# Gated mixer: mixing interleaved with the second half of u and with the output projection, which takes its first eight contraction tiles for all eight column groups at once

## The reference

```python
def gmlp_mixer(h, w_in, ln_g, ln_b, ws, bs, w_out):
    B, S, _ = h.shape                                # 1, 256, 1024
    z = jax.nn.gelu(h @ w_in, approximate=False)     # w_in: 1024 x 4096
    u, v = z[..., :GM_HALF], z[..., GM_HALF:]        # 2048 each
    v = layernorm(v, ln_g, ln_b)
    vc = v.reshape(B, S // GM_CHUNK, GM_CHUNK, GM_GROUPS, GM_GROUP_DIM)   # chunks of 128 tokens, 8 groups of 256
    mixed = jnp.einsum('gpq,bnqgc->bnpgc', ws, vc) + bs.T[None, None, :, :, None]
    return (u * mixed.reshape(B, S, GM_HALF)) @ w_out    # w_out: 2048 x 1024

x = x + g_m * gmlp_mixer(h_lat, ...)
x = x + g_f * squared_relu_mlp(modulate(x, norm_ffn_g[i], sh_f, sc_f), ffn_w1[i], ffn_w2[i])
```

## Time and profile before

| | us |
|---|---|
| median of 3 timed runs | 991.48 |
| lowest and highest of them | 991.28, 992.29 |
| span of the profiled execution, first to last instruction | 987.1 |
| median less span | 4.4 |
| PE busy in the span | 943.5 |

### The profile page before, as it was taken

One profiled execution on the slowest core, in us unless ns is written; L12 is line 12 of the kernel. 1 busy time (PEld: TensorE's weight loads), 2 busy tenths in 40 slices (PEclk: granted clock), 3 DMA queues, 4 the chain that ended last, 5 costly groups with the idle time before them and its releaser, 6 DMA issues.

```text
span 987.1 us, 19548 instructions
## 1 busy us (share of the span) xinstructions
PE 943.5 (96%) x6882; PEld 871.3 (88%) x6882; DVE 706.0 (72%) x1132; ACT 538.3 (55%) x921; POOL 309.0 (31%) x272
## 2 busy tenths in 40 slices
PE   5988989999999999999979999999999999999996
PEld 5877556799999999988969999999999879899996
DVE  4997778678988777897886688555555773475664
ACT  3464655565765444654634666654444761674645
POOL 1942122237997111120051288640110000330012
PEclk9898999999999999999979999999999998999999
DMA  9856175168878777788615676555555332255521
GB/s 351 292 182 239 42 226 171 47 218 309 309 271 275 284 267 279 244 324 283 225 61 171 234 256 214 186 176 190 171 192 182 130 95 98 86 172 173 169 87 43
DMA packets 57052, 195.60 MB, mean 198 GB/s; under 512 B 6303, under 2 KB 9791, under 8 KB 56736
## 3 DMA queue, kind: packets, MB, share of 16 engines
q1 hardware_dynamic: 55312, 192.36, 56.7%
q0 software_dynamic: 1680, 2.44, 1.1%
HBM read 192.65 MB, written 1.07 MB: 196 GB/s over the span
## 4 chain that ended last, share of the span: by engine, by line
PE 85%; DVE 9%; ACT 2%; issue 2%; DMA 1%; POOL 0%; SPq 0%; DVEq 0%; ACTq 0%
PE bank L526 24%; PE bank L527 24%; PE bank L528 24%; DVE w_lo L1576 2%; PE bank L791 1%; PE bank L925 1%; PE bank L951 1%; PE bank L624 1%; PE bank L782 1%; DMA x<-x_in 1%; PE bank L824 1%; PE bank L633 1%; PE bank L879 1%; DVE ada_raw L1678 1%; DVE ada_raw L1591 1%
## 5 line engine op out<-in xcount | busy, mean ns | idle before, releaser
L1576 DVE TENSOR_TENSOR w_lo<-raw,w_hi 128x1024 fp32r<-128x1024 f32 (+1 forms) x261 | 340.0, 1304 | 108.0 <-ACT w_hi L1146 106.1
L1146 ACT ACTIVATE w_hi<-raw 128x1024 fp32r<-128x1024 f32 (+1 forms) x261 | 272.4, 1044 | 174.4 <-PE bank L528 166.4
L526 PE MATMUL bank<-act_hi,w_hi 128*128 128x258 f32 (+1 forms) x872 | 251.5, 288 | 0.0
L527 PE MATMUL bank<-act_lo,w_hi 128*128 128x258 f32 (+1 forms) x872 | 248.0, 284 | 0.0
L528 PE MATMUL bank<-act_hi,w_lo 128*128 128x258 f32 (+1 forms) x872 | 247.5, 284 | 0.0
L526 PEld LDWEIGHTS bank<-act_hi,w_hi 128*128 128x128 f32 x872 | 166.1, 190 | 3.3 <-issue 2.8
L527 PEld LDWEIGHTS bank<-act_lo,w_hi 128*128 128x128 f32 x872 | 166.1, 190 | 1.0 <-issue 1.0
L528 PEld LDWEIGHTS bank<-act_hi,w_lo 128*128 128x128 f32 x872 | 166.1, 190 | 0.0
L528 PE MATMUL bank<-hid_hi,w_lo 128*128 128x256 f32 x512 | 143.4, 280 | 0.0
L526 PE MATMUL bank<-hid_hi,w_hi 128*128 128x256 f32 x512 | 142.8, 279 | 0.0
L527 PE MATMUL bank<-hid_lo,w_hi 128*128 128x256 f32 x512 | 142.8, 279 | 0.0
(11 more groups left out here) (349 smaller groups left out, 1812.7 us busy)
## 6 DMA issues: line engine op xcount, KB each, us to landing
raw<-weights SPq DMA_DIRECT2D x247, 512.0 KB, 3.6
ada_raw<-ada SPq DMA_DIRECT2D x88, 512.0 KB, 4.8
raw<-weights SPq DMA_DIRECT2D x14, 384.0 KB, 4.3
ada_more<-ada SPq DMA_DIRECT2D x8, 512.0 KB, 6.4
bias<-bias_by_distance SPq DMA_DIRECT2D x1, 2048.0 KB, 9.1
x<-x_in SPq DMA_DIRECT2D x1, 1024.0 KB, 7.3
ctx<-ctx_in SPq DMA_DIRECT2D x1, 1024.0 KB, 9.5
out<-result SPq DMA_DIRECT2D x4, 256.0 KB, 2.7
```

The lines of the kernel that those rows point to most:

```text
L526: pe.matmul(dst, w[0], a[0], start=start, stop=False)
L527: pe.matmul(dst, w[0], a[1], start=False, stop=False)
L1146: act.activation(w_hi[:, slot, 0:width_of(c)], raw[:, slot, 0:width_of(c)], ACT.Copy).then_inc(weight_hi, 1)
L1576: dve.tensor_tensor(w_lo[:, slot, 0:w], raw[:, slot, 0:w], w_hi[:, slot, 0:w].bitcast(fp32), ALU.subtract).then_inc(weight_lo, 1)
```

## The change

The 16 mixing tiles no longer stand in a block of their own. Tiles 0 to 7 are mixed in pairs behind groups 4 to 7 of `gm_u1`, tiles 8 to 15 one by one behind the first eight steps of `gm_out`. Mixing uses banks 4 to 7 in turn, and PE's tile t waits for DVE's tile t-4. `gm_out` is cut in two: in its first eight steps, step k takes contraction tile k for all eight output groups at once (a new order of `gm_w_out` in the chunks, `chunks_in_halves`), the groups lying two to a bank in banks 0 to 3; in its last eight steps, step 8+g takes the contraction tiles 8 to 15 of group g. `gm_out` is no longer a hardware loop. DVE makes four bias tiles in each of the steps j = 0 to 3 and two mixed tiles in each of the steps 4 to 7. The mixed tile t goes to slot (t + 8) mod 16 of `s_hi` and `s_lo`, so that tiles 0 to 7 don't write what `gm_u1` still reads.

```diff
+        def mix_slot(t):
+            return (t + 8) % 16
+        def mix_out(g):
+            return bank[(g + 2) % 4][:, g // 4 * S:(g // 4 + 1) * S]
...
 PE
-            run(project("gm_u1", 8, normed))
-            pe.wait_ge(v_normed, 2)
-            pe.wait_ge(ws_sum_ready, 2)
-            for t in range(GM // P):
-                if t >= 2:
-                    pe.wait_ge(split_src, written(split0["gm_s"] + t - 2))
+            def mix(t):
+                if t >= 4:
+                    pe.wait_ge(split_src, written(split0["gm_s"] + t - 4))
                 for n in range(2):
-                    last = pe.matmul(bank[4 + t % 2][:, n * P:(n + 1) * P], v_gm[:, n, t * P:(t + 1) * P],
+                    last = pe.matmul(bank[4 + t % 4][:, n * P:(n + 1) * P], v_gm[:, n, t * P:(t + 1) * P],
                                      ws[:, t // 2, :], start=True, stop=True)
                 last.then_inc(mixed, 1)
-            with pe.Fori(0, 2) as it:
-                run(project("gm_out", 16, lambda k: (s_hi[:, k, :], s_lo[:, k, :]), locals_=range(8),
-                            it=it, per=4, a_wait=lambda k: split0["gm_s"] + k + 1))
+            for g in project("gm_u1", 8, normed):
+                if g == 4:
+                    pe.wait_ge(v_normed, 2)
+                    pe.wait_ge(ws_sum_ready, 2)
+                if g >= 4:
+                    mix(2 * g - 8)
+                    mix(2 * g - 7)
+            c = chunk0["gm_out"]
+            for k in range(8):
+                pe.wait_ge(weight_lo, c + k + 1)
+                pe.wait_ge(split_lo, split0["gm_s"] + k + 1)
+                for g in range(KT):
+                    if k == 0 and g == 2:
+                        pe.wait_ge(evacuated, group0["gm_out"])
+                    last = split_product(mix_out(g), weight(c + k, g * P, P), mixed_act(k), k == 0 and g < 4, False,
+                                         shared=True)
+                last.then_inc(matmul_steps, 1)
+                mix(8 + k)
+            for g in range(KT):
+                pe.wait_ge(weight_lo, c + 8 + g + 1)
+                for k in range(8, 16):
+                    if g == 0:
+                        pe.wait_ge(split_lo, split0["gm_s"] + k + 1)
+                    last = split_product(mix_out(g), weight(c + 8 + g, (k - 8) * P, P), mixed_act(k), False, k == 15, shared=True)
+                last.then_inc(matmul_steps, 1)
 ACT (inside the gm_u1 loop, behind evacuate and convert; then gm_out)
-            for t in range(GM // P):
-                split(split0["gm_s"] + t, s_hi[:, t, :])
+                if g >= 4:
+                    for t in (2 * g - 8, 2 * g - 7):
+                        split(split0["gm_s"] + t, s_hi[:, mix_slot(t), :])
+            for k in range(8):
+                convert(chunk0["gm_out"] + k + 4)
+                split(split0["gm_s"] + 8 + k, s_hi[:, mix_slot(8 + k), :])
...
 DVE
-            for j in range(7):
-                for t in range(2 * j, 2 * j + (4 if j == 6 else 2)):
+            for j in range(8):
+                for t in range(0 if j >= 4 else 4 * j, 0 if j >= 4 else 4 * j + 4):
...
+                if j >= 4:
+                    mixed_tile(2 * j - 8)
+                    mixed_tile(2 * j - 7)
                 convert(chunk0["gm_u1"] + j + 4)
...
+            dve.wait_ge(evacuated, group0["gm_out"])
+            for k in range(8):
+                mixed_tile(8 + k)
+                convert(chunk0["gm_out"] + k + 4)
...
+            for g in range(KT):
+                residual("gm_out", g, mods[:, GATE2, g:g + 1], src=mix_out(g))
+                if g > 0:
+                    raw_low(RAW["ffn1_in"], g - 1, gain_column(4))
+                if g == KT - 1:
+                    raw_low(RAW["ffn1_in"], g, gain_column(4))
+                convert(chunk0["gm_out"] + 8 + g + 4)
```

More of the change, by code:

```diff
@@ L51 @@
     ("ffn0_up", [1] * 32), ("ffn0_down", [0, 0, 0, 1] * 8),
-    ("gm_u0", [1] * 8), ("gm_v", [0, 0, 0, 2] * 4), ("gm_u1", [1] * 8), ("gm_out", [0, 1] * 8),
+    ("gm_u0", [1] * 8), ("gm_v", [0, 0, 0, 2] * 4), ("gm_u1", [1] * 8), ("gm_out", [0] * 8 + [1] * 8),
     ("ffn1_up", [1] * 32), ("ffn1_down", [0, 0, 0, 1] * 8),
@@ L1655, in vec_column, with residual @@
                 return lambda o: V(name, a, KT)[:, o]
-            def residual(name, g, gate=None, it=None, groups=0, steps=0):
+            def residual(name, g, gate=None, it=None, groups=0, steps=0, src=None):
                 n = group0[name] + g
@@ L1927, in _ @@
                     modulate_loop(68 + j // 2)
-            then(ins)
-            def mixed_tile(t):
-                i = split0["gm_s"] + t
-                dst = tile_f32[:, i % 4, :].rearrange("p (n q) -> p n q", n=2)
-                dve.wait_ge(mixed, t + 1)
-                dve.wait_ge(split_lo, i - 3)
-                then(dve.scalar_tensor_tensor(dst, bank[4 + t % 2][:, 0:S].rearrange("p (n q) -> p n q", n=2),
-                                              V("gm_ln_g", t, 1),
-                                              (bs_all if t % 2 else mix_bias)[:, t // 2:t // 2 + 1, :].to_broadcast([P, 2, P]), ALU.mult, ALU.add))
-                dve.tensor_tensor(tile_f32[:, i % 4, :], tile_f32[:, i % 4, :], u_gm[:, t, :],
-                                  ALU.mult).then_inc(split_src, 1)
-            dve.wait_ge(evacuated, group0["gm_out"] - 1)
-            for t in range(GM // P):
-                if t == GM // P - 1:
-                    dve.wait_ge(evacuated, group0["gm_out"])
-                mixed_tile(t)
-                if t == 1:
-                    convert(chunk0["gm_u1"] + 11)
+            dve.wait_ge(evacuated, group0["gm_out"])
+            for k in range(8):
+                mixed_tile(8 + k)
+                convert(chunk0["gm_out"] + k + 4)
             gain_of(4, mods[:, SCALE3, :], V("norm_ffn_g", KT, KT))
             shift_low(SHIFT3, 3)
-            with dve.Fori(0, 2) as it:
-                for j in range(8):
-                    if j % 2 == 1:
-                        residual("gm_out", j // 2, mods[:, GATE2, ds(it * 4 + j // 2, 1)], it, 4, 8)
-                        raw_low(RAW["ffn1_in"], j // 2, gain_column(4), it, 4)
-                    convert(chunk0["gm_out"] + j + 4, it)
+            for g in range(KT):
+                residual("gm_out", g, mods[:, GATE2, g:g + 1], src=mix_out(g))
+                if g > 0:
+                    raw_low(RAW["ffn1_in"], g - 1, gain_column(4))
+                if g == KT - 1:
+                    raw_low(RAW["ffn1_in"], g, gain_column(4))
+                convert(chunk0["gm_out"] + 8 + g + 4)
             ffn("ffn1", 3, False, GATE3, RAW["even_in"], vec_column("norm_gain_2"))
@@ L2269, in chunks_of, with chunks_in_halves @@
     return np.concatenate([flat, np.zeros((flat.shape[0], P, CW - per * P), w.dtype)], -1)
+def chunks_in_halves(w):
+    t = tiles(w)
+    return np.concatenate([t[:, :, :KT].transpose(2, 1, 0, 3).reshape(KT, P, CW),
+                           t[:, :, KT:].reshape(KT, P, CW)])
 def chunks_by_token(w, width):
```

42 lines of the change are left out of this document (27 added, 15 removed).

## The result

The changed kernel takes 982.81 us (median of 4, 981.34 to 984.73), the kernel before 991.88 (median of 4, 991.28 to 994.74). The ratio is 0.9906, with a 95% interval from 0.9887 to 0.9926: 9.1 us less. Predicted were 981.7 us and a range from 979.0 to 985.5.

The account below looks back on a forecast made before the run. PE was taken as the bound, busy 943.5 of 987.1 us, with only the mixing block to take back. Away 21.13, back 11.3 (7.1 + 2.4 + 1.7 + 0.1): 991.48 - 9.8 = 981.7 us, range 979 to 985.5.

Parts of the forecast that it names:

- removed: The block of mixing between `gm_u1` and `gm_out` goes away: 21.13 us off PE's time.
- 16 mixing tiles: The same tiles mixed on PE between full-rate products, with nothing hiding them: 7.1 us added back.
- wait for `v_normed`: Behind group 4 of `gm_u1`, PE waits for DVE's second normalisation, delayed by six more bias tiles: 2.4 us.
- clock and evacuation: Low clock after the stall (1.65 us) and step 0's wait for `gm_u1`'s last gelu (1.0), together 1.7, the larger.
- tile 15: Mixed last, wanted by step 8 of `gm_out` as its eighth tile: cost 0.1 us, bound 0.6.
- Steps of 3.28 and 2.83 us: In `gm_out`, PE sets the pace: steps 0 to 7 take 3.28 us each, steps 8 to 15 take 2.83.
- the rival of a drain at each of the 64: Bank changes in steps 0 to 7 of `gm_out` each cost 0.16 us, 10.2 in all: 991.9 us; chance 0.03.
- The end of `gm_out` and `ffn1_up`: DVE's last low part is there when `ffn1_up` needs it: cost 0, or 0.5 us if 1 us later.
- The carry from span to median: Whole kernel: the median stands 4.4 us above the profiled span, carried over from span 977.3 to 981.7 us.
- handing-on between the engines with the clock low throughout: Rival in `gm_u1`'s second half: PE, DVE and ACT wait for each other, clock low; 984 to 987 us, chance 0.13.
- the slower case: Clock falls in the new stall and stays low through the interleaved stretch to step 7: up to 999.6 us; chance 0.03.
- The near rival: Nothing lost in the joints: clock holds, last evacuation in time; cost 10.0, 980.4 us; shares 0.76 with the forecast.

Follow-up runs that it names:

- F: Changed kernel with eight of DVE's 16 bias tiles moved behind the normalisations, into steps 0 to 3 of `gm_out`; stage 79.06 us, median 983.05 us.
- K: H with tiles 8 to 15 mixed mid-step and the eight remaining `gm_u1` bias tiles all in step 3; stage 79.15 us, median 982.83 us.
- E: Changed kernel with two extra unused PE products ahead of the wait for the normalisation, keeping PE busy; stage 80.74 us, median 982.60 us.
- G: Changed kernel with ACT's splits one group later, so a group's evacuation no longer stands behind them; stage 78.36 us, median 981.29 us.
- H: Changed kernel with the edits of F and G together; stage 77.44 us, median 978.30 us.
- D: Changed kernel with only `gm_u1` interleaved: tiles 8 to 15 mixed in one block ahead of the old `gm_out` loop; stage 88.21 us, median 989.89 us.
- A: Kernel before, with its mixing block rotating through four banks instead of two, nothing else changed; stage 84.83 us, median 985.84 us.
- B: Changed kernel with mixing back on two banks, all interleaving kept; stage 82.43 us, median 984.84 us.
- I: Changed kernel with bias tiles 4 to 9 right behind the second normalisation and 10 to 15 in step 3, within `gm_u1`; stage 82.70 us, median 982.85 us.
- C: Changed kernel with only `gm_out` interleaved: tiles 0 to 7 mixed in one block behind group 7; stage 82.01 us, median 985.05 us.

## Why the prediction was right

Counted in the trace by where each group or step starts on PE, against the same in the kernel before:

| term | predicted, us | in the trace, us |
|---|---|---|
| removed | 21.13 | 21.13 |
| 16 mixing tiles | 7.1 | 7.5 |
| wait for `v_normed` | 2.4 | 2.2 |
| clock and evacuation | 1.7 | 1.65 (1.53 + 0.12) |
| tile 15 | 0.1 | 0.64 |
| sum | -9.8 | -9.15 |

The time's share is -9.1 (medians 991.88 and 982.81).

*Removed, and the mixing between full-rate products:* right. A single tile adds 0.45 us to a step, as computed. A pair in `gm_u1` adds 1.00, since a group takes 3.72 instead of 2.72; two tiles by the sum are 0.89. The 0.11 more is not mixing. The sum took groups 5 to 7 at the old 0.113 us a product (8.15 us), and behind the new wait the 24 products of a group start 0.118 apart. The four pairs make the 0.4 us more.

*The wait for `v_normed`:* right in size and cause. Six more bias tiles of 0.26 to 0.27 each stand ahead of the second normalisation, and the wait is 2.11 us. F, which keeps four of the twelve ahead of it, has a wait of 0.42, and so has K with none.

*The evacuation and the clock, "together 1.7, the larger":* the number was right, and the rule behind it (not added, but the later of two paths) is what E, F, G and H tested and bore out. The order of the list that gave 499.2 for the gelu was right too, but it was too short. The sum has it from 486.2 to 499.2, 13.0 us; in the trace it runs from 487.56 to 502.05, 14.5 us. The difference lies mostly in three instructions of DVE beside POOL's splits, at 1.76 to 1.77 us where the sum has 1.2; I had put at most 1.1 us on that. The prediction had seen that this was possible for the converts. It missed that the reduction for the modulation (L1628) is slowed in the same way. The Trainium skill (SBUF — State Buffer, section "Who interferes with whom") puts such a slowdown on any VectorE instruction with two SBUF inputs, and so on the reduction as well; the trace agrees with 1.77 against 1.22 for it.

That the 1.7 came out is in part luck. The evacuation alone, taken at 1.0 and at most 1.5, cost 1.6 where nothing hid it (step 0 of 4.90 in E and 4.92 in F, against 3.27). It stayed out of sight because the low clock, which the changed kernel met both times and G did not, cost nearly the same. With the clock held the time would have been no better, as E shows.

*Steps of 3.28 and 2.83 us:* right to 0.01, but for step 0 (3.39) and step 8 (3.48). The bank changes cost nothing; the rival of a drain at each of the 64 would have made a step 4.6 us. The effect that the Trainium skill describes (TensorE: Matmul & The Clock Gate, section "A second HAM failure mode: psum-queue depth-cycling") does not occur in this kernel: with a new bank every three matmuls the granted clock is 1.00 in all of 501.30 to 550.87.

*Tile 15:* the mis-sized small term: 0.1 taken, 0.64 measured, just above its bound of 0.6. POOL's split takes 1.21 us beside a convert of DVE and not the 0.8 of the sum:

```profile
528.75 1.22 DVE L1613 TENSOR_TENSOR w_lo<-raw,w_hi 128x1024 fp32r<-128x1024 f32 x1
```

```profile
529.36 1.21 POOL L2163 TENSOR_TENSOR s_lo<-tile_f,s_hi 128x256 fp32r<-128x256 f32 x1 [2.07 <-ACT s_hi L1183]
```

*The end of `gm_out` and `ffn1_up`:* right; `ffn1_up` begins 0.12 us behind the last product, without a wait.

*The carry from span to median:* this step was wrong. "The median stands 4.4 us above that span, and I carry this over" took a short execution for an offset. The predicted difference was taken from the median, so the time came out right, but the span forecast by the same step, 977.3, was 3.5 too low.

*The rivals:* handing-on between the engines with the clock low throughout did not come: there was one stretch of 3.41 us. Nor did the slower case. The near rival, in which the clock holds and the evacuation is in time, was met only by G's profiled execution, with ACT's order changed.

The best kernel of the study is H: 978.30 us, 0.9866 of the kernel before [0.9842, 0.9891], 12.8 us less and 4.3 below the changed kernel.

## What to carry to other kernels

Before interleaving a block, first try to let the bound engine run further ahead in it: four banks instead of two gave more than half of the gain here. When a wait is on the bound engine, look for what ends at the same moment on the others. Here the wait and the low clock put PE 3.6 us behind, and a list on DVE ended 0.1 us later still; only with both paths shortened did the timed runs show a gain. Half an interleaving can be worse than none: D, with the part in `gm_u1` alone, is 3.4 us behind A, which has only the four banks. Work that fills a gap on another engine is free where it stands, and moving it away from there can cost more than the wait it was to cure.

## What the runs showed of the hardware

- A wait of 2.11 us on PE, at the same place behind the same products, brought the granted clock down in three executions (the changed kernel twice, and B) and left it at 1.00 in two (G and D). Where it fell it stayed at 0.50 for 3.4 us. Waits of 1.36 and 1.38 us (E, F) left it alone, one of 2.71 (I) did not. What decides at 2.11 stays open.
- In the stage a product of 256 columns starts 0.113 or 0.118 us behind the last one, both at granted clock 1.00, and the spacing changes only where PE has stood still. In all fourteen traces it is 0.113 from the start of `gm_u1` to PE's first stop and 0.118 from there on, whichever stage follows. The changed kernel has 0.118 already in groups 6 and 7 of `gm_u1`. In C a stop of 0.13 us was enough. Once it went back: in G's profiled execution, at the 0.29 us wait for tile 15, so steps 9 to 15 ran at 0.113 with the same PE instructions. The windows of PE for 16 us of those steps, in the changed kernel and then in G, show 138 against 143 records and nearly the same DMA share:

```profile
534.00:550.00 16.00, 16.00 (x138) 1.00 0.66 213
```

```profile
530.00:546.00 16.00, 16.00 (x143) 1.00 0.65 221
```

  No run here tells why.
- POOL's subtraction and a DVE instruction with two SBUF inputs hold each other up, and in these rows the one that begins later pays. The convert at 528.75 began first and kept its 1.22 us, and POOL's split took 1.21 instead of 0.80. At 492.48 POOL began first, and the convert at 492.72 took 1.76.
- Executions of one kernel differ by several us through stretches at half clock outside the stage, as in F and K above; the stage in the trace resolves edits that the medians do not.
